# Product-key experts: the first top-k block beside the query projection, operands in PSUM, one expert group kept on chip, rows earlier

## The chip, the cores and the metric

One core of a Trainium2 chip. The metric is device time in microseconds of one execution of the whole program.

## What is computed

The program is two transformer blocks over 512 tokens of width 1024 in f32. Only the last part, `peer_ffn` of the second block, is touched. For each token 8 heads each choose 16 of 16384 single-neuron experts by two top-16 searches over 128 keys and one over the 256 sums of their winners:

```python
q = jnp.einsum('bsd,de->bse', h, w_q).reshape(B, S, PEER_HEADS, PEER_D_KEY)
s1 = jnp.einsum('bshd,hnd->bshn', q[..., :PEER_HALF], keys1)
s2 = jnp.einsum('bshd,hnd->bshn', q[..., PEER_HALF:], keys2)
v1, i1 = lax.top_k(s1, PEER_TOPK)
v2, i2 = lax.top_k(s2, PEER_TOPK)
cand = (v1[..., :, None] + v2[..., None, :]).reshape(B, S, PEER_HEADS, 256)
vals, c = lax.top_k(cand, PEER_TOPK)
e1 = jnp.take_along_axis(i1, c // PEER_TOPK, axis=-1)
e2 = jnp.take_along_axis(i2, c % PEER_TOPK, axis=-1)
expert = e1 * PEER_N_KEYS + e2
gate = jax.nn.softmax(vals, axis=-1)
# per token: act = gelu(h . u_tab[expert]);  out = sum(gate * act * v_tab[expert])
```

## The kernel before, in words

**Two ways for the tokens.** Tokens 128 to 511 (384 of them, `DENSE`) take a dense way: the activations of all 16384 experts are computed, and a gate matrix that is zero off the chosen experts multiplies them. Tokens 0 to 127 take the sparse way: their 128 experts each are fetched as rows of 4 KB per token, 128 rows of the first table (`u_rows`, dot products) and 128 of the second (`v_rows`, weighted sums), one row for each token per fetch (512 KB).

**Weight tiles.** All matrix products run over a list of tiles of 128x1024 f32. SyncE loads tile t into one of 3 places (`raw`) once the low half of tile t-3 is made. ScalarE (or, before the first expert table, GpSimd) copies it rounded into `wH` (L1114), GpSimd subtracts into `wL` (L1628) once tile t-2 is done on TensorE, and TensorE makes 24 products for a tile (high x high, high x low, low x high, 8 parts; L1643 to L1645). The last 256 tiles are the two expert tables, 16 groups of 8 tiles each.

**Order of the work around the change.**
1. *Query projection*, 16 tiles (`wq`), all 512 tokens. VectorE and ScalarE normalise the tokens beside it. All three compute engines meet after it (`E.meet()`).
2. *Top-k stage.* 32 units, one per block of 128 tokens and head. For unit u TensorE makes the key scores (`key_scores`, L909, one unit ahead, released by `tk_read`), and `BESIDE` says how many tiles of the first table it then does. VectorE runs each unit's searches (L1472 to L1486) with the candidate sum at L1479; the last unit of a block also turns choices into expert numbers and gates (L1492 to L1519, with the searches L1501, L1504, L1505 over 2048 elements, twice). After block 0 the rows of the first table can be fetched; from unit 9 on VectorE takes 3 of them at the start of a unit (`take_row`, L1452), 69 in all. Experts and gates of blocks 1 to 3 are turned to expert-major order (`turn_slots`, `keep_slots`).
3. *Gate stage.* 96 steps of 4 tokens: VectorE makes one-hot rows (L1530) and gated one-hot rows (L1533, four per step), TensorE multiplies them (`gate_products`, L948), three banks in turn, and ScalarE copies the product out (L1150); every 8 steps a store of 2 MB goes to memory. Beside them 36 tiles of the first table, 3 per 8 steps, and 28 dot rows.
4. *Rest of the first table*, 6 tiles. Each finished tile of the first table goes through gelu on ScalarE (L1121) and is stored to memory (L1124).
5. *Second table*, 16 groups of 8 tiles. For each expert tile activations (`Ga`, loads of half a group, L1173) and gates (`Gt`, L1166) come back from memory, ScalarE copies the activation to PSUM (L1180), VectorE multiplies (L1557), both split the result into high and low parts (L1203, L1545), one group ahead of TensorE; VectorE adds each finished tile to the tokens (L1564). Beside it come the last 31 dot rows, over the first 23 tiles, and the 128 rows of the second table (L1459), over the next 93.

**Row fetches.** GpSimd issues them (L1619) in its one queue, right behind the low half of the tile that `ROWS_AFTER` names, 3 tiles before the use. There are 6 places; the fetch of row o waits until row o-6 is used:

```python
if o >= ROWS_HELD:
    pool.wait_ge(sems("rows_used"), o - ROWS_HELD + 1)
```

Of the kernel before, what the change touches and what calls it, by code (L numbers as in the profile page):

```python
# [19 lines left out]
P = 128  # L20
# [135 lines left out]
class Chain:  # L156
# [52 lines left out]
def build(nc, a, first=True, second=True):  # L209

    with ExitStack() as ctx:
# [44 lines left out]
        def over(spec, inner=()):  # L256

            with ExitStack() as e:
                got = {n: sb(n, s, d, on=e) for n, s, d in spec}
                for more in inner:  # L260
# [381 lines left out]
        def second_pe(E, products, products_and_sums, parts_ready, one_tile, part_of_tile, rows_tile, turn, h_hi, h_lo):  # L642
# [255 lines left out]
            E.meet()  # L898
# [3 lines left out]
            pe.wait_ge(sems("keys_in"), 16)  # L902

# [1625 lines left out]
```

## Time and profile before

| | us |
|---|---|
| median of 3 runs (3072.8, 3075.3, 5824.1) | 3075.3 |
| the profiled execution | 3079.0 |
| its span | 3077.3 |

| engine | busy us | share of the span |
|---|---|---|
| PE (TensorE) | 2909.5 | 95% |
| DVE (VectorE) | 2064.6 | 67% |
| POOL (GpSimd) | 1758.3 | 57% |
| ACT (ScalarE) | 1008.4 | 33% |

The mean granted clock of TensorE is 0.989. The stages above lie at about 1680 to 1767 us (projection), 1767 to 2172 (top-k), 2172 to 2412 (gates), 2412 to 2445, and 2445 to 3074 (second table).

How to read it: in a row of windows stand the stretch in us and its length; then the busy us, with instructions in brackets, of PE, PEld (weight loads of TensorE, beside its products), DVE, ACT and POOL; then the granted clock, the mean busy share of the 16 DMA engines, and GB/s. A timeline row has its start and duration in us, the engine, the line, the operation and its tiles; in brackets the idle time before it and what ended it. A wait for several things is put down to the last of them.

### The profile page before, as it was taken

How to read it: one execution, taken by the hardware profiler on the slowest of the kernel's cores; microseconds unless marked ns; L12 is line 12 of the kernel's file. 1: busy time of each engine (PE TensorE's matmuls, PEld its weight loads, DVE VectorE, ACT ScalarE, POOL GpSimd, SP SyncE). 2: the span in 40 equal slices, each digit the busy share in tenths (PEclk: the TensorE clock that was granted, in tenths of full speed). 3: DMA queues.
4: the chain of work that ended last, by engine and by line, in shares of the span. 5: the costliest groups of instructions: out<-in, count | busy, mean ns of one | idle time of the engine just before them, and what ended most of it. 6: DMA issues, size and time to landing. Idle time of an engine off the chain costs nothing.

```text
span 3077.3 us, 40592 instructions
## 1 busy us (share of the span) xinstructions
PE 2909.5 (95%) x15510; PEld 2574.9 (84%) x15510; DVE 2064.6 (67%) x3546; ACT 1008.4 (33%) x1596; POOL 1758.3 (57%) x997
## 2 busy tenths in 40 slices
PE   6999999999999999999999999999999899888889
PEld 5777778888787788788888899999999788888889
DVE  7985369994433625755566299999999366666664
ACT  2152222221222422233321132333566434333333
POOL 4636457776654155411156647877544477777775
PEclk9998999999999999999999999999999999999999
DMA  3212222332232022200033348778677899999995
GB/s 137 89 62 89 69 70 95 97 99 94 88 109 76 28 83 88 72 18 15 15 110 104 95 151 295 258 260 280 226 283 276 298 317 335 331 329 332 334 332 178
DMA packets 201521, 509.15 MB, mean 165 GB/s; under 512 B 15600, under 2 KB 98800, under 8 KB 199792
## 3 DMA queue, kind: packets, MB, share of 16 engines
q1 hardware_dynamic: 73008, 262.64, 25.8%
q0 software_dynamic: 36864, 134.23, 11.9%
q10 hardware_dynamic: 91456, 109.68, 11.1%
q8 instruction: 124, 2.03, 0.3%
q14 instruction: 69, 0.57, 0.1%
HBM read 451.97 MB, written 54.53 MB: 165 GB/s over the span
## 4 chain that ended last, share of the span: by engine, by line
PE 63%; POOL 14%; DVE 12%; issue 7%; ACT 2%; DMA 1%; ACTq 0%; DVEq 0%; POOLq 0%; SPq 0%
PE banks L1643 16%; PE banks L1645 15%; PE banks L1644 15%; POOL sb_wL L1628 9%; DVE sb_sq L2356 3%; POOL sb_rows L1619 3%; PE banks L948 3%; PE banks L406 2%; PE banks L822 1%; POOL sb_tmp L1619 1%; PE banks L830 1%; DVE sb_tmp L2366 1%; DVE sb_sq L2354 1%; PE banks L1679 1%; PE banks L1705 1%
## 5 line engine op out<-in xcount | busy, mean ns | idle before, releaser
L1610 POOL TENSOR_TENSOR sb_wL<-sb_raw,sb_wH 128x1024 fp32r<-128x1024 f32 x242 | 588.4, 2431 | 878.9 <-PE banks L1645 817.4
L1643 PE MATMUL banks<-sb_hH,sb_wH 128*128 128x512 f32 (+1 forms) x2040 | 765.5, 375 | 30.3 <-POOL sb_wL L1628 18.7
L1628 POOL TENSOR_TENSOR sb_wL<-sb_raw,sb_wH 128x1024 fp32r<-128x1024 f32 x253 | 624.0, 2468 | 255.9 <-PE banks L1645 247.0
L1644 PE MATMUL banks<-sb_hL,sb_wH 128*128 128x512 f32 (+1 forms) x2040 | 743.3, 364 | 0.0
L1645 PE MATMUL banks<-sb_hH,sb_wL 128*128 128x512 f32 (+1 forms) x2040 | 743.2, 364 | 0.0
L1643 PEld LDWEIGHTS banks<-sb_hH,sb_wH 128*128 128x128 f32 x2040 | 387.1, 190 | 82.5 <-POOL sb_wL L1628 22.1
L1643 PE MATMUL banks<-sb_pzH,sb_wH 128*128 128x384 f32 x1024 | 354.5, 346 | 74.0 <-POOL sb_wL L1628 68.1
L1645 PEld LDWEIGHTS banks<-sb_hH,sb_wL 128*128 128x128 f32 x2040 | 386.2, 189 | 40.8
L1644 PEld LDWEIGHTS banks<-sb_hL,sb_wH 128*128 128x128 f32 x2040 | 387.4, 190 | 38.7 <-issue 1.7
L1114 ACT ACTIVATE sb_wH<-sb_raw 128x1024 fp32r<-128x1024 f32 x253 | 267.3, 1057 | 312.7 <-DMA sb_raw<-in_weights 271.7
L1645 PE MATMUL banks<-sb_pzH,sb_wL 128*128 128x384 f32 x1024 | 345.2, 337 | 0.0
L1644 PE MATMUL banks<-sb_pzL,sb_wH 128*128 128x384 f32 x1024 | 345.0, 337 | 0.0
L1605 POOL TENSOR_SCALAR sb_wH<-sb_raw 128x1024 fp32r<-128x1024 f32 x242 | 305.1, 1261 | 13.0 <-DMA sb_raw<-in_weights 13.0
L1643 PEld LDWEIGHTS banks<-sb_pzH,sb_wH 128*128 128x128 f32 x1024 | 193.6, 189 | 99.7 <-POOL sb_wL L1628 83.2
L1564 DVE TENSOR_TENSOR sb_xT<-sb_xT,banks 128x384 f32<-128x384 f32 x128 | 71.0, 555 | 234.6 <-PE banks L1645 234.2
L1644 PEld LDWEIGHTS banks<-sb_pzL,sb_wH 128*128 128x128 f32 x1024 | 194.1, 190 | 0.0
L1645 PEld LDWEIGHTS banks<-sb_pzH,sb_wL 128*128 128x128 f32 x1024 | 193.7, 189 | 0.0
L1121 ACT ACTIVATE sb_sq<-banks 128x384 f32<-128x384 f32 x128 | 64.8, 506 | 267.1 <-PE banks L1645 262.0
L2356 DVE SCALAR_TENSOR_TENSOR sb_sq<-sb_uab,sb_params,sb_sq 128x512 f32<-128x512 f32 x88 | 145.4, 1652 | 3.1
L1150 ACT ACTIVATE sb_stage<-banks 128x512 f32<-128x512 f32 x96 | 108.7, 1132 | 86.3 <-PE banks L948 84.4
L1533 DVE TENSOR_SCALAR sb_gated<-banks,sb_slots 128x128 f32<-128x128 f32 x384 | 130.6, 405 | 0.0
L1619 POOL DMA_INDIRECT sb_rows<-in_v_rows,sb_idx x86 | 81.3, 946 | 74.3 <-DVE banks L1459 66.7
(456 smaller groups left out, 5222.2 us busy)
## 6 DMA issues: line engine op xcount, KB each, us to landing
sb_raw<-in_weights SPq DMA_DIRECT2D x495, 512.0 KB, 3.6
acts<-sb_sq ACTq DMA_DIRECT2D x128, 192.0 KB, 4.0
gates<-sb_stage ACTq DMA_DIRECT2D x12, 2048.0 KB, 7.9
sb_Ga<-acts ACTq DMA_DIRECT2D x32, 768.0 KB, 7.5
sb_Gt<-gates ACTq DMA_DIRECT2D x32, 768.0 KB, 10.2
acts<-sb_xT ACTq DMA_DIRECT2D x1, 2048.0 KB, 7.8
sb_xT<-acts ACTq DMA_DIRECT2D x1, 2048.0 KB, 10.1
out_xT<-sb_xT ACTq DMA_DIRECT2D x8, 256.0 KB, 2.5
```

The source lines that it names most:

```text
L948: mm = pe.matmul(ps[2 + r][:, x * P:(x + 1) * P], B["gated"][:, i % 4, x], B["onehot"][:, i % 4, x], start=True, stop=True)
L1114: act.activation(wH[:, t % HIS, :], raw[:, t % RAWS, :], ACT.Copy).then_inc(sems("weights_hi"), 1)
L1150: act.activation(stage[:, :, 4 * r:4 * r + 4].rearrange("p e t -> p t e"), ps[2 + i % 3][:, :].rearrange("p (t e) -> p t e", t=4), ACT.Cop ...
L1533: ins = v.tensor_scalar(B["gated"][:, r, x], iota, at(1, x), at(2, x), ALU.is_equal, ALU.mult)
L1605: nc.gpsimd.tensor_scalar(wH[:, t % HIS, :], raw[:, t % RAWS, :], 1.0, 0.0, ALU.mult, ALU.add).then_inc(sems("weights_hi"), 1)
L1610: nc.gpsimd.tensor_tensor(wL[:, t % LOS, :], raw[:, t % RAWS, :], wH[:, t % HIS, :].bitcast(F32), ALU.subtract).then_inc(sems("weights_lo" ...
L1619: nc.gpsimd.indirect_dma_start(out=rows_at[o % ROWS_HELD], out_offset=None, in_=a["u_rows"] if o < P else a["v_rows"], in_offset=bass.Indi ...
L1628: nc.gpsimd.tensor_tensor(wL[:, t % LOS, :], raw[:, t % RAWS, :], wH[:, t % HIS, :].bitcast(F32), ALU.subtract).then_inc(sems("weights_lo" ...
L1643: pe.matmul(out, hi, H, start=start, stop=False)
L1644: pe.matmul(out, hi, L, start=False, stop=False)
L1645: return pe.matmul(out, lo, H, start=False, stop=stop)
L2356: ins = v.scalar_tensor_tensor(out=to, in0=u[:, k:S + k], scalar=PM("ffn_w", wcol + k), in1=to, op0=ALU.mult, op1=ALU.add)
```

## The change

- Units 0 to 6 move beside the projection: `SCORES_BESIDE` places their scores within its tiles, in banks 6 and 7. The meeting after the projection is dropped for single waits. `BESIDE` starts at unit 7 (`FIRST_UNIT`); 87 tiles instead of 86 lie in the top-k stage and 38 instead of 36 in the gate stage.
- One operand of the candidate sum and of the two searches over 2048 moves to PSUM (`first_in_bank`, `iota`, `if12`); each unit has one small copy more for it.
- A gate step makes its rows with three operations over 512 elements, one of them to PSUM (`equal`), instead of one over 512 and four over 128; the products have two banks instead of three.
- 126 instead of 69 dot rows lie in the top-k stage (5 or 6 per unit from unit 9), the last 2 at the start of the gate stage, then 32 rows of the second table; 96 are left for the second table.
- The last group of the first table is taken first in the second (`GROUP_ORDER`); its activations go straight to `Ga` and its gates to `Gt`, and neither is stored or loaded.

```diff
-BESIDE = ((1, 2, 1, 2, 1, 2, 1, 7),) + 3 * ((2, 2, 3, 2, 2, 2, 3, 7),)
-TOPK_TILES = sum(map(sum, BESIDE))
+FIRST_UNIT = 7
+BESIDE = (6,) + 3 * (3, 2, 3, 3, 2, 3, 3, 8)
+TOPK_TILES = sum(BESIDE)
-GATE_TILES = 3 * GATE_STEPS // 8
+GATE_TILES = 38
+SCORES_BESIDE = {(7, 0): 0, (7, 4): 1, (8, 4): 2, (9, 4): 3, (11, 4): 4, (13, 4): 5, (15, 4): 6}
+GROUP_ORDER = [GROUPS - 1] + list(range(GROUPS - 1))
+KEPT = P - 8
-UNIT_DOTS = {u: (3 * (u - 9), 3 * (u - 9) + 3) for u in range(9, 32)}
-GATE_DOTS = [69 + 28 * i // GATE_STEPS for i in range(GATE_STEPS + 1)]
-LATE_ROWS = [97 + 31 * min(i, 23) // 23 if i < 25 else 128 + 128 * min(i - 25, 93) // 93 for i in range(121)]
-DOTS_DONE = 23
+EARLY_DOTS = 126
+UNIT_DOTS = {u: (EARLY_DOTS * (u - 9) // 23, EARLY_DOTS * (u - 8) // 23) for u in range(9, 32)}
+DOTS_DONE = 8
+GATE_ROWS = [EARLY_DOTS + min(i, DOTS_DONE) * (P - EARLY_DOTS) // DOTS_DONE + max(i - DOTS_DONE - 2, 0) * 32 // 86 for i in range(GATE_STEPS + 1)]
+LATE_ROWS = [GATE_ROWS[-1] + (2 * P - GATE_ROWS[-1]) * i // 118 if i < 118 else 2 * P for i in range(121)]
+GATE_AT = [8 * GATE_TILES * (i + 1) // GATE_STEPS - 1 for i in range(GATE_STEPS)]
...
+        work, cand = kept[:, 0, 0:256], kept[:, 0, 256:512]
+        iota, if12 = ps[5][:, 0:P], ps[5][:, P:3 * P].rearrange("p (h c i) -> p h c i", h=8, c=2)
+        v12, first_in_bank = [kept[:, 1, 16 * c:16 * c + 16] for c in range(2)], ps[5][:, 3 * P:3 * P + 16]
...
             def beside_wq(b, k):
+                if (b, k) in SCORES_BESIDE:
+                    first_scores(SCORES_BESIDE[b, k])
...
-            E.meet()
+            first_scores(FIRST_UNIT)
+            E.at("rb_used", E.n["made rb"])
...
-                r = i % 3
+                r = i % 2
                 E.eng.wait_ge(sems("gb_rows"), i + 1)
-                E.at("gb_copied", i - 2)
+                E.at("gb_copied", i - 1)
...
+                if n >= KEPT:
+                    act.activation(B["Ga"][:, n - KEPT, :], bank(t, DN), ACT.Gelu).then_inc(sems(f"bank_free{BANK[t]}"), 1)
+                    weight_hi(t + HIS)
+                    return
...
-                act.activation(stage[:, :, 4 * r:4 * r + 4].rearrange("p e t -> p t e"),
-                               ps[2 + i % 3][:, :].rearrange("p (t e) -> p t e", t=4), ACT.Copy).then_inc(sems("gb_copied"), 1)
+                product = ps[2 + i % 2][:, :].rearrange("p (t e) -> p t e", t=4)
+                act.activation(stage[:, 0:KEPT, 4 * r:4 * r + 4].rearrange("p e t -> p t e"), product[:, :, 0:KEPT], ACT.Copy)
+                act.activation(B["Gt"][:, j, :, 4 * r:4 * r + 4].rearrange("p e t -> p t e"), product[:, :, KEPT:P],
+                               ACT.Copy).then_inc(sems("gb_copied"), 1)
...
+                    if c == 0:
+                        chain.after(v.tensor_copy(first_in_bank, vals))
-                chain(v.tensor_tensor(cand, B["v12"][:, 0].unsqueeze(2).to_broadcast([P, 16, 16]),
-                                      B["v12"][:, 1].unsqueeze(1).to_broadcast([P, 16, 16]), ALU.add))
+                chain(v.tensor_tensor(cand.rearrange("p (i j) -> p i j", i=16), first_in_bank.unsqueeze(2).to_broadcast([P, 16, 16]),
+                                      v12[1].unsqueeze(1).to_broadcast([P, 16, 16]), ALU.add))
...
-                chain(v.tensor_copy(B["if12"][:], B["i12"][:]))
+                chain(v.tensor_copy(if12, B["i12"][:]))
-                                          C("iota", 0, 16).unsqueeze(1).to_broadcast([P, P, 16]), ALU.is_equal))
+                                          iota[:, 0:16].unsqueeze(1).to_broadcast([P, P, 16]), ALU.is_equal))
-                    chain(v.tensor_tensor(e4, e4, B["if12"][:, :, c].unsqueeze(2).to_broadcast([P, 8, 16, 16]), ALU.mult))
+                    chain(v.tensor_tensor(e4, e4, if12[:, :, c].unsqueeze(2).to_broadcast([P, 8, 16, 16]), ALU.mult))
...
+            equal = ps[4][:, :].rearrange("p (x t) -> p x t", x=4)
-                v.tensor_tensor(B["onehot"][:, r], iota.unsqueeze(1).to_broadcast(bc),
-                                B["slots"][:, 0, 4 * i:4 * i + 4].unsqueeze(2).to_broadcast(bc), ALU.is_equal)
-                for x in range(4):
-                    ins = v.tensor_scalar(B["gated"][:, r, x], iota, at(1, x), at(2, x), ALU.is_equal, ALU.mult)
-                ins.then_inc(sems("gb_rows"), 1)
-                for o in range(GATE_DOTS[i], GATE_DOTS[i + 1]):
+                E.at("gb_rows", i)
+                chain.after(v.tensor_tensor(equal, iota.unsqueeze(1).to_broadcast(bc), slot(1), ALU.is_equal))
+                v.tensor_tensor(B["onehot"][:, r], iota.unsqueeze(1).to_broadcast(bc), slot(0), ALU.is_equal)
+                chain.wait()
+                v.tensor_tensor(B["gated"][:, r], equal, slot(2), ALU.mult).then_inc(sems("gb_rows"), 1)
+                for o in range(GATE_ROWS[i], GATE_ROWS[i + 1]):
                     take_row(o)
...
-    peer = [u.reshape(-1, P, D), d.reshape(-1, P, D)]
+    peer = [u.reshape(-1, P, D), d[GROUP_ORDER].reshape(-1, P, D)]
```

## Rows read from the trace of the kernel before

**Rows 1.** Windows of the whole core; the columns are named under time and profile.

```profile
1680.00:1767.00 87.00, 85.95 (x384) 70.52 (x385) 19.23 (x26) 15.19 (x26) 53.93 (x31) 1.00 0.32 102
1767.00:2172.00 405.00, 386.34 (x2226) 382.74 (x2225) 383.63 (x1000) 137.72 (x189) 297.84 (x159) 0.97 0.72 245
2172.00:2412.00 240.00, 237.35 (x1633) 237.00 (x1633) 215.40 (x536) 153.54 (x170) 109.98 (x61) 0.99 0.74 263
2412.00:2452.00 40.00, 32.76 (x172) 30.23 (x170) 7.27 (x14) 16.95 (x29) 22.47 (x13) 0.91 0.98 353
2452.00:3074.00 622.00, 553.65 (x3062) 529.97 (x3062) 378.57 (x562) 235.17 (x369) 446.85 (x279) 0.99 0.91 312
1875.00:1900.00 25.00, 25.00 (x148) 24.81 (x147) 23.66 (x73) 8.73 (x12) 21.96 (x16) 1.00 0.97 352
```

**Rows 2.** Timeline of VectorE: start us, us, line, operation, [idle before <-releaser].

```profile
3070.06 0.56 DVE L1564 TENSOR_TENSOR sb_xT<-sb_xT,banks 128x384 f32<-128x384 f32 x1 [3.61 <-PE banks L1645]
3074.22 0.56 DVE L1564 TENSOR_TENSOR sb_xT<-sb_xT,banks 128x384 f32<-128x384 f32 x1 [3.61 <-PE banks L1645]
```

**Rows 3.** Timeline of ScalarE's queue and of TensorE between the two tables.

```profile
2427.77 6.39 ACTq L1166 DMA_DIRECT2D sb_Gt<-gates  x2
...
2445.43 0.66 PE L1643 MATMUL banks<-sb_pzH,sb_wH 128*128 128x384 f32 x1 [5.36 <-POOL sb_wL L1628]
```

**Rows 4.** Waits, 2475 to 3020: who for whom, us in total, times, longest us.

```profile
POOL sb_rows L1619 <- DVE banks L1459: 66.7, 45, 2.6
PE banks L1643 <- POOL sb_wL L1628: 61.5, 63, 1.3
```

**Rows 5.** Timeline of GpSimd in the second table.

```profile
2634.12 0.94 POOL L1619 DMA_INDIRECT sb_tmp<-in_v_rows,sb_idx  x1 [1.26 <-DVE banks L1459]
2635.07 2.39 POOL L1628 TENSOR_TENSOR sb_wL<-sb_raw,sb_wH 128x1024 fp32r<-128x1024 f32 x1
```

**Rows 6.** Transfers from 2590 to 3010: all queues' packets, and the weight tiles.

```profile
DMA packets 73479, 139.43 MB, mean 332 GB/s; under 512 B 3911, under 2 KB 47661, under 8 KB 73452
...
sb_raw<-in_weights SPq DMA_DIRECT2D x85, 512.0 KB, 6.2
```

**Rows 7.** Gate stage: VectorE's timeline; durations (ns min/median/max, first, last start).

```profile
2296.87 1.21 DVE L1452 SCALAR_TENSOR_TENSOR sb_tmp<-sb_tmp,banks 128x1024 f32<-128x1024 f32 x1
...
2298.00 0.69 DVE L1530 TENSOR_TENSOR sb_onehot<-banks,sb_slots 128x512 f32<-128x512 f32 x1
2298.61 1.36 DVE L1533 TENSOR_SCALAR sb_gated<-banks,sb_slots 128x128 f32<-128x128 f32 x4
2299.89 0.69 DVE L1530 TENSOR_TENSOR sb_onehot<-banks,sb_slots 128x512 f32<-128x512 f32 x1
...
L948 PE MATMUL banks<-sb_onehot,sb_gated x768: 271/275/423, 2176.9 to 2412.4; 128*128 128x128 f32 x192
...
L1530 DVE TENSOR_TENSOR sb_onehot<-banks,sb_slots x96: 682/692/704, 2174.9 to 2402.9; 128x512 f32<-128x512 f32 x96
```

**Rows 8.** Top-k: units 0 and 1 start on VectorE; durations, sum and search.

```profile
1767.46 0.30 DVE L1472 MAX8 sb_v<-banks 128x8 f32<-128x128 f32 x1 [0.47 <-PE banks L909]
...
1774.15 0.30 DVE L1472 MAX8 sb_v<-banks 128x8 f32<-128x128 f32 x1
...
L1479 DVE TENSOR_TENSOR sb_cand<-sb_v x32: 424/466/4381, 1771.2 to 2144.0; 128x256 f32<-128x256 f32 x32
...
L1504 DVE TENSOR_TENSOR sb_eq<-sb_eq,sb_if x8: 2293/4369/4378, 1829.2 to 2162.3; 128x2048 f32<-128x2048 f32 x8
```

**Rows 9.** Timeline of VectorE, its first operation after the projection.

```profile
1766.69 0.29 DVE L1443 COPY banks<-sb_consts 128x128 f32<-128x128 f32 x1 [39.74 <-ACTq L200]
```

**Rows 10.** Row fetches from 1850 to 2170, from issue to landing.

```profile
DMA to landing us min/median/max: 4.7/6.5/7.5
```

**Rows 11.** Timeline of TensorE behind a wait at the end of top-k.

```profile
2166.84 0.51 PE L1643 MATMUL banks<-sb_hH,sb_wH 128*128 128x384 f32 x1 [2.48 <-POOL sb_wL L1628]
2167.15 0.52 PE L1644 MATMUL banks<-sb_hL,sb_wH 128*128 128x384 f32 x1
```

More of the change, by code:

```diff
@@ L92 @@
     for _o in range(_a, _b):
-        ROWS_AFTER[_o] = sum(BESIDE[n // 8][n % 8] for n in range(_u)) - ROWS_AHEAD
+        ROWS_AFTER[_o] = sum(BESIDE[:_u - FIRST_UNIT]) - ROWS_AHEAD
 for _i in range(GATE_STEPS):
-    for _o in range(GATE_DOTS[_i], GATE_DOTS[_i + 1]):
-        ROWS_AFTER[_o] = TOPK_TILES + 3 * _i // 8 - ROWS_AHEAD
+    for _o in range(GATE_ROWS[_i], GATE_ROWS[_i + 1]):
+        ROWS_AFTER[_o] = TOPK_TILES + GATE_AT[_i] // 8 - ROWS_AHEAD
 for _i in range(120):
@@ L161, in __init__, with after, wait, __call__ @@
         self.eng, self.sem, self.n = eng, sem, 0
-    def __call__(self, ins):
+    def after(self, ins):
         ins.then_inc(self.sem, 1)
         self.n = self.n + 1
+    def wait(self):
         self.eng.wait_ge(self.sem, self.n)
+    def __call__(self, ins):
+        self.after(ins)
+        self.wait()
 class Side:
@@ L884, in second_pe, with score_bank, key_scores, first_scores @@
             products("out2", 8, h_hi, h_lo, ready=lambda k: E.wait("merged_parts"))
+            def score_bank(u):
+                return ps[6 + u % 2 if u < 8 else 2 + u % 2]
+            def key_scores(u):
+                tb, h = u // 8, u % 8
+                E.at("tk_read", 2 * (u - 1))
+                for c in range(2):
+                    mm = pe.matmul(score_bank(u)[:, c * P:(c + 1) * P], B["qp"][:, 2 * h + c, tb * P:(tb + 1) * P],
+                                   B["keys"][:, 2 * h + c, :], start=True, stop=True)
+                mm.then_inc(sems("tk_scores"), 1)
+            def first_scores(h):
+                if h == 0:
+                    pe.wait_ge(sems("keys_in"), 16)
+                for c in range(2):
+                    emptied(E, TILE["wq"] + 2 * h + c)
+                key_scores(h)
             def beside_wq(b, k):
+                if (b, k) in SCORES_BESIDE:
+                    first_scores(SCORES_BESIDE[b, k])
                 if b == 0:
@@ L1103, in second_act @@
                     hi_part(E, hH[:, k, :])
-            E.meet()
+            E.at("sq_used", E.n["made sq"])
             t0 = TILE["peer"]
@@ L1132, in second_act @@
             n = 0
-            for u in range(32):
-                for b in range(BESIDE[u // 8][u % 8]):
-                    if b == 3:
+            for u in range(FIRST_UNIT, 32):
+                for b in range(BESIDE[u - FIRST_UNIT]):
+                    if u % 8 == 7 and b == (2 if u == 7 else 4):
                         E.wait("tk_centred")
```

136 lines of the change are left out of this document (64 added, 72 removed).

## The prediction, before the result was known

> **What bounds the kernel now.** First the span by stages [rows 1]; in each row the reader is to see who is busy to the brim. In the query projection (1680 to 1767) TensorE is, while VectorE works 19 of 87 us. In the top-k stage (1767 to 2172, 86 tiles) it is VectorE: 384 of 405 us. In the gate stage (2172 to 2412, 36 tiles, 96 steps) it is TensorE again. From 2412 to 2452 the granted clock is 0.91, and in the second table (2452 to 3074) no engine is full: TensorE 554 of 622 us, VectorE 379, GpSimd 447, with the DMA engines at 0.91.
>
> A tile without waits is read at the end, where adds that each wait for a tile start 4.16 us apart [rows 2]. 128 tiles would be 532 us; the second table takes 629 (from 2445.4, [rows 3], to about 3074). The waits [rows 4] say why: TensorE waits for the low half of the weights (L1628), and GpSimd, which makes it, waits for VectorE's use of rows (L1459, 66.7 us in one of two groups). In GpSimd's queue [rows 5] the row fetch of 2634.12 waits 1.26 us and the weight half stands right behind it. A row is fetched 3 tiles ahead into 6 places; at 128 rows in 93 tiles (1.37) a place's last use lies 4.4 tiles before its next, so the fetch waits for a tile just ended. The tile is 4.94 us there (85 in 420 us, [rows 6]).
>
> **The second table after.** The change leaves it 96 rows over 118 tiles, 0.81 a tile; a place is then used 7.4 tiles before its next use, and the fetch stops waiting. What is late next: GpSimd has 2.4 + 0.81 x 0.95 = 3.2 us a tile [rows 5], VectorE and ScalarE less than now, so the transfers. A tile moves 0.524 MB of weights, 0.393 of activations and gates and 0.43 of rows, 1.34 MB; at the 332 GB/s that this stretch reaches [rows 6] that is 4.05 us, below 4.16, and in [rows 1] a stretch with DMA share 0.97 has TensorE at 25.00 of 25. I take 4.20 us, between 4.16 (nothing shows) and 4.35 (bursts of two 768 KB loads show): 128 x 4.20 = 538 us.
>
> **Between the tables.** Now two gate loads keep ScalarE's queue 6.39 us, and TensorE waits 5.36 us [rows 3]. After, the last group's activations and gates stay in their buffers and that group is taken first: its product, split and transfer to the operand run behind the last three tiles of the first table. I leave 1 us for the last part, gelu to split.
>
> **Gate stage.** The gate products run from 2176.9 to 2412.4 [rows 7]; less 36 tiles that leaves 0.9 us for each of 96 steps. With 38 tiles: 235.5 + 8.3 = 244 us, if TensorE still bounds. VectorE now needs 1.89 us a step (2298.00 to 2299.89) and 1.13 a dot row (2296.87 to 2298.00). After, it has three operations over 512 instead of one and four over 128; one over 512 lets the next start 0.61 us later (2298.00 to 2298.61), so 1.83, and 0.15 for two waits on its own results. With 2 dot rows and 32 rows of the second table, priced at the 1.21 of a dot row's duration, that is 190 + 41 = 231 us, under 244: covered by TensorE. The new operations write or read PSUM on both sides; between no more (0.61) and twice that, only the upper end would bind, by up to 176 us less the cover of 13; I take the row's value, since L1530 already reads PSUM. The gate copy on ScalarE is split in two and has two banks instead of three: it may then be late by two steps, 5 us; covered.
>
> **Top-k on VectorE.** A unit without rows is 1767.46 to 1774.15, 6.69 us, and holds a candidate sum of the shortest kind; over the stage this sum takes 0.42 to 4.38 us, and the search L1504 2.29 to 4.38 [rows 8]. Both have two operands in SBUF. L1530, with one in PSUM, stays at 0.68 to 0.70 in 96 calls [rows 7]. The change puts one operand of each in PSUM, so I take the shortest times: a unit 6.69 plus a small copy of 0.18 (between nothing and a short max of 0.30), 6.87; the end of a block six operations of 2.32 and 2.6 of small ones, 16.5; and 6 us in all for two small operations that keep both operands in SBUF (between nothing and 8 x 4.4).
>
> Units 0 to 6 move beside the projection. VectorE is free there from 1766.69 - 39.74 = 1727.0 [rows 9]; a projection tile is 24 x 87 / 384 = 5.44 us. Scores 2 are due in tile 8 at 1726.0 but need unit 0 read (3.0 us into the unit, 1730.4); scores 3, at 1736.3, need unit 1 (1737.3): TensorE waits 5.4 us. Seven pairs of score products add 7 x 0.45. The first table starts at 1775.6 instead of about 1771, and VectorE starts unit 7 at 1778.8, as the scores of unit 6 come at 1771.9. From there it has 25 x 6.87 + 126 x 1.14 + 4 x 16.5 + 6 = 388 us; TensorE has 87 x 4.16 + 24 x 0.45 + 6 = 379. VectorE still bounds, by little.
>
> **What 57 more rows cost in that stage.** A unit that doesn't end a block has 2.71 tiles and 5.5 rows: VectorE 13.1 us, TensorE 11.7. It moves 2.71 x 0.721 + 5.5 x 0.524 = 4.84 MB: 13.3 us at the 352 GB/s and 0.97 of the dense stretch [rows 1], 14.6 at 332 [rows 6]. I take 13.5, near the first, which is of this stage: 0.4 over VectorE in 20 units, 8 us. The Trainium skill gives a core about 358 GB/s of HBM (DMA: Bandwidth & Descriptors, Specifications). An estimate by that rule is 13.5 us for this unit, no ground to move the sum; the trace's 352 at share 0.97 agrees.
>
> Then the queue. The rows of a unit can be fetched only as those of the unit before are used, and the weight half behind them needs 0.95 + 2.4 us more. TensorE can't come nearer to VectorE than about 9 us at a unit of two tiles and 5 at one of three; being faster it will be there, so the last unit's tiles (8 x 4.16 + 0.45 from 4.7 us after VectorE's start) end 8.6 us after VectorE's work.
>
> **Sum.** VectorE ends top-k at 1778.8 + 388 + 8 = 2174.8, TensorE at 2183.4 (now about 2173). The first gate product comes 4 us later, as now, then 244, three tiles 12.5, and 1: the second table starts at 2444.9, as now, but without the stumbling start. 538 us is 2982.9, and 3.4 from the last product to the end: span 2986 against 3077.3. The profiled execution took 3079.0; the median of the runs shown is 3075.3, 2 under the span. The forecast is **2984 us**, 3.0% less.
>
> **Rivals.**
> - *The top-k stage waits for rows* (16%). For it: three engines within 4% of each other there, six places for 5.5 rows a unit. Against: rows land in 7.5 us at most in that stage [rows 10], and a place has about 13. At 14.6 to 15 us a unit, 20 units cost 22 to 30 more: 3006 to 3014.
> - *The second table stays at the transfers' bound* (10%), at 4.40 us a tile: 26 us more, 3010. For it is the DMA share of 0.91 over the whole stage; against, the 4% below TensorE.
> - *PSUM operands don't help* (9%): the long times of L1479 and L1504 have another cause. By the stage's own 24 sums and the searches, 24 x 0.8 + 6 x 2.1 = 32 us come back: 3016.
> - *Slower* (7%): GpSimd, blocked behind rows that VectorE frees in bursts of 5.5 x 1.14 = 6.3 us, holds the weight half over 8.3 us (two tiles) in the top-k stage. TensorE then stands, and its clock is low after it: behind a wait of 2.48 us its products start 0.32 us apart [rows 11], against 4.16 / 24 = 0.17. 6 us of waiting and 2 of the low clock in 23 units is 184, of which 30 are in my sum: 3138. It decides once VectorE leads TensorE by less than 5 us. Against: scores are made a unit ahead, so VectorE can lead by a unit.
>
> That the rows don't move as said is excluded by the tables in the diff.
>
> **Numbers.** Forecast 58%, its own range 2966 (4.16 a tile, no transfer term) to 3005 (4.30 and 16 us). Faster by over 2%, about what a measurement of this kernel can tell from no change, means under 3013.8: the 58, and half or a little less of the three rivals near that line, 74%. Same 19%, slower 7%. The range 2955 to 3030 leaves out the slow case and ends of the others.
>
> **What would show it.** In the changed profile: adds 4.2 us apart in the second table, GpSimd not waiting for VectorE there, DMA share over 0.95; no gap of TensorE over 2 us between the tables; no candidate sum over 0.5 us; VectorE over 95% busy in top-k. Wrong would be: row products waiting for transfers in top-k, weight halves over 8 us behind fetches, tiles of 4.4 us in the second table.

## The result, and the profile after

The changed kernel takes 3053.3 us (median of 6 runs, 3048.6 to 3058.8) against 3074.1 before: ratio 0.9935, 95% interval 0.9921 to 0.995. (The 3074.1 is a median over six runs too, one of which took 5824.1; the ratio leaves that one out.) That is 0.65% faster, clear of noise by its interval but under the 2% that the prediction counted as a change; the forecast was 3.0%, 2984 us, with a range of 2955 to 3030. The profiled execution took 3053.7, its span is 3051.8.

Three times divide a span: the first gate product, the last one, the end.

| kernel | first gate product | gate stage | last gate product to the end | span |
|---|---|---|---|---|
| before | 2176.9 | 235.5 | 664.9 | 3077.3 |
| forecast | 2187 | 244 | 555 | 2986 |
| after | 2246.3 | 243.9 | 561.6 | 3051.8 |

So 59 of the 66 us by which the span misses the forecast went in the top-k stage and 7 behind the gate stage. Windows of the whole core after: top-k stage, gate stage, the 40 us between the tables, second table [against rows 1].

```profile
1775.00:2242.00 467.00, 412.49 (x2215) 406.16 (x2214) 375.40 (x970) 138.68 (x191) 326.13 (x216) 0.92 0.77 276
2246.00:2490.00 244.00, 243.73 (x1669) 243.74 (x1670) 217.09 (x323) 155.97 (x265) 119.13 (x69) 0.99 0.73 267
2490.00:2530.00 40.00, 31.14 (x165) 30.02 (x165) 15.10 (x27) 20.03 (x37) 21.15 (x12) 0.87 0.83 286
2530.00:3048.00 518.00, 518.00 (x2993) 517.96 (x2992) 291.23 (x455) 229.63 (x355) 383.44 (x215) 1.00 0.88 303
```

In the last row TensorE is never idle; in the first nobody is full: TensorE 412 of 467 us at a clock of 0.92, VectorE 375, GpSimd 326, transfers at 0.77. So here the time goes in waits of one queue for another, and the next step is to find which. The second table and the gate stage came as forecast: adds 4.16 us apart [as rows 2], 128 of them in 530.4 us; candidate sums and searches always at their shortest [rows 8]; the 96 steps of the gate stage with 0.70, 0.68 and 0.68 us for the three operations [rows 7].

VectorE's adds, then durations (ns min/median/max) of the adds, the sum, a search and the gate stage's new operation:

```profile
3044.65 0.55 DVE L1609 TENSOR_TENSOR sb_xT<-sb_xT,banks 128x384 f32<-128x384 f32 x1 [3.61 <-PE banks L1687]
3048.81 0.55 DVE L1609 TENSOR_TENSOR sb_xT<-sb_xT,banks 128x384 f32<-128x384 f32 x1 [3.61 <-PE banks L1687]
...
L1609 DVE TENSOR_TENSOR sb_xT<-sb_xT,banks x128: 553/554/555, 2518.4 to 3048.8; 128x384 f32<-128x384 f32 x128
...
L1518 DVE TENSOR_TENSOR sb_dg<-banks,sb_dg x32: 424/424/426, 1726.9 to 2207.1; 128x256 f32<-128x256 f32 x32
...
L1543 DVE TENSOR_TENSOR sb_eq<-sb_eq,banks x8: 2286/2286/2290, 1789.2 to 2222.5; 128x2048 f32<-128x2048 f32 x8
...
L1571 DVE TENSOR_TENSOR banks<-banks,sb_slots x96: 689/700/700, 2244.3 to 2480.2; 128x512 f32<-128x512 f32 x96
```

What holds the top-k stage is in its waits, 1775 to 2242 (who for whom, us in total, times, longest us):

```profile
POOL sb_wL L1670 <- PE banks L1687: 98.8, 40, 5.1
PEld banks L1685 <- POOL sb_wL L1670: 60.7, 21, 3.9
PE banks L1685 <- POOL sb_wL L1670: 54.5, 21, 3.5
DVE sb_rows L1490 <- DMA sb_rows<-in_u_rows,sb_idx: 37.7, 30, 4.4
POOL sb_rows L1661 <- issue: 18.6, 63, 0.3
DVE sb_tmp L1490 <- DMA sb_tmp<-in_u_rows,sb_idx: 16.2, 14, 4.9
```

TensorE waits 21 times for a low half, up to 3.5 us, about once a unit. VectorE waits 54 us for rows, but GpSimd hardly ever for VectorE. GpSimd's own timeline at one such place, and TensorE's behind it:

```profile
1825.59 2.41 POOL L1670 TENSOR_TENSOR sb_wL<-sb_raw,sb_wH 128x1024 fp32r<-128x1024 f32 x1 [2.28 <-PE banks L1687]
1828.14 0.95 POOL L1661 DMA_INDIRECT sb_tmp<-in_u_rows,sb_idx  x1
1829.40 0.94 POOL L1661 DMA_INDIRECT sb_tmp<-in_u_rows,sb_idx  x1 [0.30 <-issue]
1830.64 0.94 POOL L1661 DMA_INDIRECT sb_rows<-in_u_rows,sb_idx  x1 [0.30 <-issue]
1831.89 0.94 POOL L1661 DMA_INDIRECT sb_rows<-in_u_rows,sb_idx  x1 [0.31 <-issue]
1833.13 0.94 POOL L1661 DMA_INDIRECT sb_rows<-in_u_rows,sb_idx  x1 [0.30 <-issue]
1834.38 0.94 POOL L1661 DMA_INDIRECT sb_rows<-in_u_rows,sb_idx  x1 [0.30 <-issue]
1835.32 4.71 POOL L1670 TENSOR_TENSOR sb_wL<-sb_raw,sb_wH 128x1024 fp32r<-128x1024 f32 x2
```

```profile
1837.75 0.44 PE L1685 MATMUL banks<-sb_hH,sb_wH 128*128 128x384 f32 x1 [3.53 <-POOL sb_wL L1670]
1838.03 0.38 PE L1686 MATMUL banks<-sb_hL,sb_wH 128*128 128x384 f32 x1
1838.20 0.53 PE L1687 MATMUL banks<-sb_hH,sb_wL 128*128 128x384 f32 x1
1838.52 0.53 PE L1685 MATMUL banks<-sb_hH,sb_wH 128*128 128x384 f32 x1
```

The reader is to see that nothing in this burst waits for another engine: the fetches start 1.24 us apart, 0.94 of the record and 0.30 that the trace calls issue. The first low half starts when a tile ends (1825.5); its place in `wL` was the one that tile freed, so TensorE has from there just two tiles and a pair of scores, until 1834.2. GpSimd needs low half, six fetches, low half, until 1837.7. TensorE stands 3.53 us, and 0.45 us later (1838.20) its products start 0.32 us apart instead of 0.17, until 1841.4: the granted clock of that stretch is 0.50, the 1.2 GHz level instead of 2.4.

**Theory A**: GpSimd's queue, a low half behind a burst of fetches, is the cost. **Theory B**: the transfers (266 to 361 GB/s in stretches of this stage, VectorE waiting for rows) are. **Theory D**: something else in the change is. For the 7 us between the tables the question is whether an order or the transfers make them.

### The profile page after: what moved, and what is told of

Same layout as the page of the kernel before. It is cut to its first block, busy times and chain, and to the rows that moved or that the text cites. A ratio compares the mean times of both kernels' runs of the same rounds, so it can differ in the third digit from the quotient of the medians.

```text
span 3051.8 us, 40601 instructions
## 1 busy us (share of the span) xinstructions
PE 2911.1 (95%) x15510; PEld 2598.6 (85%) x15510; DVE 2022.2 (66%) x3386; ACT 1011.1 (33%) x1692; POOL 1735.4 (57%) x997
## 4 chain that ended last, share of the span: by engine, by line
PE 76%; DVE 12%; POOL 5%; issue 4%; ACT 2%; DMA 1%; DVEq 0%; ACTq 0%; SPq 0%; POOLq 0%
PE banks L1685 20%; PE banks L1687 19%; PE banks L1686 19%; DVE sb_sq L2398 3%; PE banks L978 3%; POOL sb_wL L1670 3%; POOL sb_rows L1661 2%; PE banks L839 2%; PE banks L423 1%; PE banks L847 1%; DVE sb_tmp L2408 1%; DVE sb_sq L2396 1%; PE banks L1747 1%; POOL sb_tmp L1661 1%; PE banks L1721 1%
## 5 line engine op out<-in xcount | busy, mean ns | idle before, releaser
L1652 POOL TENSOR_TENSOR sb_wL<-sb_raw,sb_wH 128x1024 fp32r<-128x1024 f32 x242 | 588.5, 2432 | 881.3 <-PE banks L1687 829.9
L1685 PE MATMUL banks<-sb_hH,sb_wH 128*128 128x512 f32 (+1 forms) x2040 | 775.1, 380 | 65.2 <-POOL sb_wL L1670 54.5
L1670 POOL TENSOR_TENSOR sb_wL<-sb_raw,sb_wH 128x1024 fp32r<-128x1024 f32 x253 | 606.5, 2402 | 354.7 <-PE banks L1687 351.2
L1686 PE MATMUL banks<-sb_hL,sb_wH 128*128 128x512 f32 (+1 forms) x2040 | 752.7, 369 | 0.0
L1685 PE MATMUL banks<-sb_pz,sb_wH 128*128 128x384 f32 x1024 | 343.4, 335 | 7.5 <-DVE sb_pz L1590 7.5
L1686 PE MATMUL banks<-sb_pz,sb_wH 128*128 128x384 f32 x1024 | 343.0, 335 | 0.0
L1687 PE MATMUL banks<-sb_pz,sb_wL 128*128 128x384 f32 x1024 | 342.9, 335 | 0.0
L1685 PEld LDWEIGHTS banks<-sb_pz,sb_wH 128*128 128x128 f32 x1024 | 192.9, 188 | 8.4 <-DVE sb_pz L1590 8.4
L1686 PEld LDWEIGHTS banks<-sb_pz,sb_wH 128*128 128x128 f32 x1024 | 192.9, 188 | 0.0
L1687 PEld LDWEIGHTS banks<-sb_pz,sb_wL 128*128 128x128 f32 x1024 | 192.9, 188 | 0.0
L1490 DVE SCALAR_TENSOR_TENSOR sb_rows<-sb_rows,banks 128x1024 f32<-128x1024 f32 x86 | 103.5, 1220 | 40.2 <-DMA sb_rows<-in_u_rows,sb_idx 37.7
L1195 ACT ACTIVATE sb_stage<-banks 128x480 f32<-128x480 f32 x96 | 102.2, 1065 | 82.1 <-PE banks L978 80.5
L1497 DVE SCALAR_TENSOR_TENSOR banks<-sb_rows,sb_row_weights,banks 128x1024 f32<-128x1024 f32 x85 | 109.0, 1282 | 0.0
```

Source lines behind the costliest of these rows:

```text
L1195: act.activation(stage[:, 0:KEPT, 4 * r:4 * r + 4].rearrange("p e t -> p t e"), product[:, :, 0:KEPT], ACT.Copy)
L1490: ins = v.scalar_tensor_tensor(out=row, in0=row, scalar=1.0, in1=row_bank, op0=ALU.mult, op1=ALU.mult, accum_out=B["dots"][:, o:o + 1])
L1497: ins = v.scalar_tensor_tensor(out=row_bank, in0=row, scalar=B["row_weights"][:, o - P:o - P + 1], in1=row_bank, op0=ALU.mult, op1=ALU.add)
L1652: nc.gpsimd.tensor_tensor(wL[:, t % LOS, :], raw[:, t % RAWS, :], wH[:, t % HIS, :].bitcast(F32), ALU.subtract).then_inc(sems("weights_lo" ...
L1670: nc.gpsimd.tensor_tensor(wL[:, t % LOS, :], raw[:, t % RAWS, :], wH[:, t % HIS, :].bitcast(F32), ALU.subtract).then_inc(sems("weights_lo" ...
L1685: pe.matmul(out, hi, H, start=start, stop=False)
```

## The experiments

**e1, a quarter of the bytes.** 

> From row 6 on a fetch moves a quarter of a row for each token (128 KB instead of 512 KB), so the rows' values are wrong and the dot products are multiplied by zero; the number of fetches, their places in GpSimd's queue and VectorE's instructions are those of the changed kernel. Theory A (GpSimd's queue: 5 or 6 fetches at 1.24 us each and then the low half stand in a row, 9.8 us against two tiles' 8.3): the top-k stage (from the scores of unit 7 at 1773 to the last turn at 2242, 469 us) stays within 10 us of 469, TensorE goes on waiting about 3.5 us for a low half once in each unit. Theory B (the transfers, up to 361 GB/s in this stage, hold rows and weight tiles up): the stage loses at least 40 us, and the waits for low halves fall under 20 us in all, from 54. The second table stays at 4.16 us a tile either way, since TensorE was never idle there.

```diff
+                full = rows_at[o % ROWS_HELD]
+                table = a["u_rows"] if o < P else a["v_rows"]
                 nc.gpsimd.indirect_dma_start(
-                    out=rows_at[o % ROWS_HELD], ...
+                    out=full if o < ROWS_HELD else full[:, 0:D // 4], out_offset=None,
+                    in_=table if o < ROWS_HELD else table.rearrange("n (q d) -> (n q) d", q=4), ...
```

One run, 3052.0 us; first gate product 2252.0, last 2495.9. The same window and waits as above:

```profile
1775.00:2242.00 467.00, 408.83 (x2211) 401.72 (x2210) 373.85 (x990) 137.32 (x190) 328.03 (x216) 0.93 0.55 174
...
L1663 POOL DMA_INDIRECT sb_rows<-in_u_rows,sb_idx x86: 941/949/1137, 1807.7 to 2246.6; - x86
...
PE banks L1688 <- POOL sb_wL L1673: 57.4, 21, 3.6
```

174 GB/s instead of 276 and nothing is gained: B falls for this stage, and by waits that stay alike (57.4 and 54.5 us in 21), not only by the time of a single run. A fetch of a quarter costs GpSimd as much, 949 ns against 937. The Trainium skill (Perfetto Trace Analysis, DMA Instruction — SWDGE (GPSIMD)) says that the record of such a DMA ends when its descriptors are generated, not when the data has moved; the trace agrees. Behind the gate stage this kernel needs 554.3 us instead of 561.6, which comes back below.

**e2, the same rows, spread.** 

> The same rows in the same units, but at most two fetches behind the low half of one tile instead of 5 or 6. Theory A (queue): TensorE's waits for low halves fall from 54 us to under 15, the granted clock of the stage rises from 0.92 to over 0.96, the top-k stage falls from 469 us to 400 to 430, the program to 2985 to 3015. Theory B (transfers): as many bytes in as short a time, so the stage stays at 455 to 469 and the program at 3040 to 3055. Rival C: the last fetches of a unit now come too late for VectorE, its waits for rows grow from 54 us, and GpSimd then waits for used places; the stage gains less than 15 us or loses.

```diff
... (against the changed kernel)
-        ROWS_AFTER[_o] = sum(BESIDE[:_u - FIRST_UNIT]) - ROWS_AHEAD
+        ROWS_AFTER[_o] = sum(BESIDE[:_u - FIRST_UNIT]) - ROWS_AHEAD + (_o - _a) // 2
```

Median 2996.0 us of 4 (2990.1 to 3003.4), ratio to before 0.9742 (0.9708 to 0.9777). First gate product at 2183.2, 63 us earlier; window and waits of the stage:

```profile
1775.00:2179.00 404.00, 385.11 (x2187) 378.28 (x2186) 366.99 (x950) 142.10 (x191) 327.14 (x214) 0.98 0.89 318
...
PE banks L1685 <- POOL sb_wL L1670: 18.7, 18, 3.6
```

(The profiled run is the fastest of the four; by the medians the gain is 57 us.) One term in one line is worth 1.9%. A holds, though 18.7 us of waits stay where under 15 were expected; C is out, as VectorE's waits for rows fall from 54 to 16 us. The 18.7 are of the same kind: in six places, where the last fetch of a unit of two tiles meets the first of the next unit, the edit still puts three or four fetches behind one low half and not two, and 14.6 us of the waits end 6 to 9 us after the first fetch of one of these six. Before the longest, 3.56 us at 1854.3, the three fetches start at 1845.93, 1847.19 and, after 2.77 us in which GpSimd waits for VectorE's use of a row, 1850.90.

**e4, no rows moved.** 

> Everything of the change but the rows' move: 69 dot rows in the top-k stage (3 per unit), 28 in the gate stage, 31 dot rows and all 128 rows of the second table beside it, as before the change. Theory A (queue): 3 fetches and a low half are 6.1 us, under two tiles' 8.3; TensorE does not wait, the stage is TensorE's own 87 tiles and scores, 385 to 400 us. Rival D (something else in the change holds the stage up: one operand in PSUM, two banks of scores, 8 tiles in the last unit): it stays above 430 us. The second table goes back to about 4.9 us a tile, 620 to 628 us, so the program is near 3050 either way under A (70 to 80 us gained in top-k, 80 to 85 lost in the second table: 3040 to 3065) and near 3110 to 3130 under D.

```diff
-EARLY_DOTS = 126
-DOTS_DONE = 8
+EARLY_DOTS = 69
+DOTS_DONE = 23
-GATE_ROWS = ...
-LATE_ROWS = ...
+GATE_ROWS = [69 + 28 * i // GATE_STEPS for i in range(GATE_STEPS + 1)]
+LATE_ROWS = [97 + 31 * min(i, 23) // 23 if i < 25 else 128 + 128 * min(i - 25, 93) // 93 for i in range(121)]
```

with `row_weights` made at step 8 + 23 + 1 of the second table, as before the change. Median 3046.9 of 4, ratio 0.9908 (0.9875 to 0.994); first gate product 2155.2, last 2399.0, 646.1 from there to the end.

```profile
1775.00:2151.00 376.00, 375.25 (x2196) 371.98 (x2196) 302.24 (x843) 140.03 (x191) 273.88 (x157) 1.00 0.77 263
...
PE banks L1685 <- POOL sb_wL L1670: 0.7, 3, 0.3
DVE sb_rows L1490 <- DMA sb_rows<-in_u_rows,sb_idx: 31.8, 24, 4.9
DVE sb_tmp L1490 <- DMA sb_tmp<-in_u_rows,sb_idx: 7.7, 9, 1.8
```

TensorE is busy in 375.25 of 376 us at full clock, D is out, and VectorE waits 39.5 us for rows all the same: here it is early, and that wait costs nothing. In the traces the rows' move costs 91.1 us before the gate stage (2155.2 to 2246.3) and brings 84.5 behind it (646.1 to 561.6): as it was done, the largest part of the change lost 7 us. (The medians say the same, 3046.9 against 3053.3, but their intervals overlap: whether it lost a little or nothing is not shown.) The rest of the change moved the first gate product from 2176.9 to 2155.2.

**e6 and e7, the size of the burst.** 

> Only how many rows stand in one burst is changed: 92 dot rows in the top-k stage, 4 per unit, all behind one low half; 34 dots in the gate stage, 2 dots and all 128 rows of the second table beside it, so only the top-k stage is read. Theory A: 4 fetches and a low half are 4 x 1.24 + 2.4 = 7.4 us, still under two tiles' 8.3, so TensorE waits under 5 us in the stage and the first gate product is at 2155 to 2160. Rival E (the rows cost in proportion to their number, 91 us for 57 rows more): 23 rows more than 69 cost 37 us, 2192.

```diff
-EARLY_DOTS = 69
+EARLY_DOTS = 92
-GATE_ROWS = [69 + 28 * i // GATE_STEPS ...
-LATE_ROWS = [97 + 31 * min(i, 23) // 23 ...
+GATE_ROWS = [92 + 34 * i // GATE_STEPS ...
+LATE_ROWS = [126 + 2 * min(i, 23) // 23 ...
```

(against e4.) 

> 115 dot rows in the top-k stage, 5 in every unit's burst (the changed kernel: 11 units of 5 and 12 of 6); 13 dots and 26 rows of the second table in the gate stage, 102 beside the second table. Theory A: 5 x 1.24 + 2.4 = 8.6 us against 8.3, so each burst costs TensorE a wait of 0.3 to 2 us and now and then its clock; first gate product at 2175 to 2215. Rival E (proportional): 2155.2 + 46 x 1.6 = 2229.

```diff
-EARLY_DOTS = 126
-DOTS_DONE = 8
+EARLY_DOTS = 115
+DOTS_DONE = 24
```

One run of each, 3061.4 and 3028.7 us in all. TensorE's waits for low halves from 1775 to 2246, e6 and then e7, in a fence each:

```profile
PE banks L1685 <- POOL sb_wL L1670: 21.9, 23, 1.5
```

```profile
PE banks L1685 <- POOL sb_wL L1670: 42.5, 21, 2.7
```

| rows in a burst | waits, us | longest | 2 x 2.4 + 1.24 r - 8.32 | first gate product | later than e4 |
|---|---|---|---|---|---|
| 3 (e4) | 0.7 | 0.3 | 0.2 | 2155.2 | |
| 4 (e6) | 21.9 | 1.5 | 1.4 | 2188.2 | 33 |
| 5 (e7) | 42.5 | 2.7 | 2.7 | 2222.2 | 67 |
| 5 or 6 (after) | 54.5 | 3.5 | 2.7 or 3.9 | 2246.3 | 91 |

Here my own sum was wrong: with one low half in it (7.4 us against 8.3) four fetches should have been free, and I expected 2155 to 2160 for e6 and 2175 to 2215 for e7. The timeline above has two low halves in the two tiles, the one before the burst and the one behind it; with both the sum, made after these runs, gives the longest wait of e4, e6 and e7 and that of the changed kernel to 0.4 us. Rival E, in proportion to the rows, gave 2192 and 2229 and was nearer to the time, but e2 refutes it as a cause: 57 rows more than e4, spread, cost 28 us instead of 91 (34 by e2's median).

The waits are 21, 42 and 54 us more than e4's, and 12, 25 and 37 us are left over. In e7 and in the changed kernel most of that is the low clock behind the waits: the stage's clock is 0.95 and 0.92, and 131 and 187 products start 0.32 us apart instead of 0.17, which makes 19 and 27 us. In e6, whose waits are 1.5 us at most, the clock is 1.00 and not one product does; its 12 us are something else. About half is the restart of each wait: round one of 1.07 us (1837.73) the products' starts are 1.41 us apart, and the next 0.28, where 0.17 is the rule, so 0.28 us more are lost than the wait shows: 6 us in 23 waits, and about as much in e7, where it closes the sum (19 + 6 for 25). What is left, some 6 us in e6 and 4 in the changed kernel, is open.

**e3, two orders between the tables.** 

> Two orders are changed between the tables: ScalarE copies the kept activations up before it makes the next weight tile's high half, and VectorE makes the low part of expert tile 7 before it waits for the gates of the next group. If the two waits of TensorE of 3.8 us each at 2511.9 and 2517.0 came from these orders, both vanish, the program is 8 to 12 us shorter (ratio to the changed kernel 0.996 to 0.997) and the clock in the 25 us after is at its full value. If they come from the load of the gates or the weight tile itself (the transfers), the waits stay and move by less than 1 us; then the program is the same within 2 us.

```diff
... (ScalarE; early_gelu(n, False) leaves out its weight_hi)
-                    while n < 8 * GROUPS and n <= KEPT + m + 2:
-                        early_gelu(n)
-                        n += 1
+                    late = n < 8 * GROUPS and n <= KEPT + m + 2
+                    if late:
+                        early_gelu(n, False)
+                        n += 1
                     if m + 2 < 8 * GROUPS:
                         act_up(m + 2)
+                    if late:
+                        weight_hi(t0 + n - 1 + HIS)
... (VectorE; the weighted_lo(m - 1) further down is left out for m == 8)
+                if m == 8:
+                    weighted_lo(7)
                 if z < GROUPS:
                     if z and e % 4 == 0:
                         E.eng.wait_ge(sems(f"gates_in{e // 4}"), 16 * z)
```

Median 3044.9 of 4, ratio 0.9903 (0.987 to 0.9937), which overlaps that of the changed kernel. In the traces, from the last gate product to the end, 556.5 us instead of 561.6; the other 5.8 us of the two traces' difference lie before the first gate product, which this edit does not touch. So the 8.4 us between the medians, which would fit the 8 to 12 expected, are not all the edit's: 5 are seen where it works. After had two waits in its first tile of the second table (first fence, with a window of 10 us ahead of them); the second fence is e3's, which has one:

```profile
2500.00:2510.00 10.00, 8.12 (x47) 7.80 (x45) 2.04 (x4) 5.24 (x10) 7.53 (x5) 1.00 1.00 367
...
2508.80 1.06 ACT L1148 ACTIVATE sb_wH<-sb_raw 128x1024 fp32r<-128x1024 f32 x1 [3.28 <-DMA sb_raw<-in_weights]
...
2511.89 0.69 PE L1685 MATMUL banks<-sb_pz,sb_wH 128*128 128x384 f32 x1 [3.77 <-DVE sb_pz L1590]
2517.00 0.69 PE L1685 MATMUL banks<-sb_pz,sb_wH 128*128 128x384 f32 x1 [3.77 <-DVE sb_pz L1590]
```

```profile
2503.27 1.06 ACT L1148 ACTIVATE sb_wH<-sb_raw 128x1024 fp32r<-128x1024 f32 x1 [3.06 <-DMA sb_raw<-in_weights]
...
2505.35 0.44 PE L1691 MATMUL banks<-sb_pz,sb_wH 128*128 128x384 f32 x1 [3.07 <-DVE sb_pz L1594]
```

Half of each theory: the order of VectorE cost one wait; the other stays, since ScalarE's next split stands behind a high half whose raw tile has not landed, while the transfers are full (the window of after, share 1.00). e1, with the old orders and fewer bytes, has 554.3, and its two waits there are 2.17 and 0.36 us. So these orders cost what they do because the transfers are full there.

**e5, rows divided by GpSimd's room.** 

> Rows are divided by GpSimd's room: 116 in the top-k stage (4 per unit, 12 in a block's last unit), of a unit's fetches at most two behind one low half, VectorE takes them in twos and fours between the searches; 34 in the gate stage (12 dots, then 22 rows), 106 beside the second table; the two orders of e3 are in it. Theory A (GpSimd's queue per block: 27 low halves at 2.4 us and 40 fetches at 1.24 us are 114 us, under TensorE's 118): TensorE waits under 8 us in the top-k stage, first gate product at 2155 to 2170 (with 69 rows 2155.2, with 126 spread rows 2183.2), gate stage 244 us, second table 556.5 us after the last gate product plus 0 to 10 for ten rows more there: 2958 to 2980. Theory B (transfers hold the stage up once rows and tiles come together, up to 361 GB/s): first gate product at 2175 to 2190, waits for low halves or for raw tiles of 15 us and more, 2980 to 2995.

```diff
+TOPK_ROWS = {u: 12 if u % 8 == 7 else 4 for u in range(9, 32)}
-EARLY_DOTS = 126
+EARLY_DOTS = sum(TOPK_ROWS.values())
-DOTS_DONE = 8
+DOTS_DONE = 32
-...max(i - DOTS_DONE - 2, 0) * 32 // 86...
+...max(i - DOTS_DONE - 2, 0) * 22 // 62...
-        ROWS_AFTER[_o] = sum(BESIDE[:_u - FIRST_UNIT]) - ROWS_AHEAD
+        ROWS_AFTER[_o] = sum(BESIDE[:_u - FIRST_UNIT]) - ROWS_AHEAD + (_o - _a) * BESIDE[_u - FIRST_UNIT] // (_b - _a)
```

with `take_rows(2)` before a unit's searches, 2 after them, and in a block's last unit 4 after each of its two searches over 2048. The two orders of e3 are in it. Median 2962.0 of 5 (2959.1 to 2967.2), ratio 0.9644 (0.9631 to 0.9658).

```profile
1775.00:2162.00 387.00, 382.72 (x2241) 381.03 (x2240) 363.97 (x970) 143.99 (x193) 323.97 (x209) 1.00 0.91 323
...
L979 PE MATMUL banks<-sb_onehot,sb_gated x768: 272/275/418, 2165.6 to 2409.5; 128*128 128x128 f32 x192
...
2560.00:2800.00 240.00, 240.00 (x1386) 240.00 (x1385) 148.03 (x227) 108.79 (x173) 188.00 (x111) 1.00 0.96 334
```

3.6% less than before, 3.0% less than the changed kernel. TensorE waits 3.5 us for low halves in the whole stage, with at most two fetches behind any one and transfers at 323 GB/s: A. The end is 555.5 us behind the last gate product.

**e8, its operands back in SBUF.** 

> e5 with the operands of the candidate sum and of the two searches over 2048 back in SBUF. By the rows of before against those of the changed kernel VectorE loses 0.5 us on each of 23 sums and 2.1 us on each of 6 pairs of searches, 24 us in the stage. If VectorE still has room beside TensorE (with 69 rows it was busy 169 of 200 us), the program is within 6 us of e5; if VectorE and GpSimd now lie on TensorE's path because GpSimd's low halves are also held while VectorE reads, first gate product 15 to 30 us later than in e5.

```diff
... (against e5)
-                        chain.after(v.tensor_copy(first_in_bank, vals))
-first_in_bank.unsqueeze(2)...    iota[:, 0:16].unsqueeze(1)...    if12[:, :, c].unsqueeze(2)...
+v12[0].unsqueeze(2)...           C("iota", 0, 16).unsqueeze(1)... B["if12"][:, :, c].unsqueeze(2)...
```

Median 2995.2 of 4, ratio 0.9762 (0.9745 to 0.9779): 33 us slower than e5. First gate product 2195.6 against 2165.6. Durations of the sum, then waits from 1775 to 2145:

```profile
L1528 DVE TENSOR_TENSOR sb_dg<-sb_dg x32: 424/1717/2285, 1724.2 to 2151.2; 128x256 f32<-128x256 f32 x32
...
PE banks L1700 <- POOL sb_wL L1685: 23.1, 10, 7.9
POOL sb_rows L1676 <- DVE sb_rows L1495: 16.4, 7, 8.5
POOL sb_tmp L1676 <- DVE sb_tmp L1495: 12.2, 3, 8.5
```

The sum's median goes from 0.42 to 1.72 us, VectorE falls behind, and now GpSimd does wait for used places, up to 8.5 us, with low halves behind it, for which TensorE then waits up to 7.9 us. PSUM operands are worth 30 us here; in e4 VectorE has 74 of 376 us free, so it was not measured what they are worth there. The Trainium skill (SBUF — State Buffer, SBUF: two separate sides) says that a VectorE operation with two SBUF inputs and a GpSimd operation that reads SBUF exclude each other for a whole instruction; the sums agree with it: 424 ns at the shortest and 2285 at the longest, 1.86 us more, which is under the 2.4 us of one low half.

**e9, fewer rows at the end.** 

> e5 with 6 rows fewer in unit 31 (6 instead of 12), taken beside the second table instead (112 there); the rest as in e5. In e5 TensorE waits once, 3.4 us, for a low half and once, 2.6 us, for the gated rows near 2150, and its first gate product is at 2165.6 against 2155.2 with 69 rows. If VectorE's 6 rows of 1.3 us in unit 31 hold the last experts and gates up, the first gate product comes 5 to 9 us earlier, 2157 to 2161, and the second table stays at TensorE's 4.16 us a tile: 2953 to 2958, ratio to e5 0.997 to 0.999. If 112 rows there are past what the transfers carry (0.96 of their time was used with 106 rows), the second table takes 5 us or more longer, and the time is that of e5 or worse.

```diff
... (against e5)
-TOPK_ROWS = {u: 12 if u % 8 == 7 else 4 for u in range(9, 32)}
+TOPK_ROWS = {u: 4 + (8, 8, 2)[u // 8 - 1] * (u % 8 == 7) for u in range(9, 32)}
```

The profiled run did a little more than expected: first gate product 2154.4, 11 us earlier, 2953.2 us. But the five runs go from 2953.2 to 2968.8, median 2967.0, ratio 0.9652 (0.9639 to 0.9666), that of e5. Four of five have a mean clock of 0.992 to 0.995 where the profiled one has 0.998; only that one has a trace. So the 11 us rest on one trace of each kernel, e5's from the slower end of its five runs and e9's from the fastest; whether the edit gains anything there, and what takes it back, is open.

**e10, more beside the second table.** 

> e5 with 101 rows in the top-k stage (7 instead of 12 in a block's last unit), 34 in the gate stage and 121 beside the second table; only the second table is read. A tile there moves 1.05 MB of weights, activations and gates (524 + 197 + 197 KB are 0.92 MB) and 121/118 rows of 524 KB, 1.455 MB in all. If the transfers' bound is the 332 to 337 GB/s at which the second table of before ran, that is 4.32 to 4.38 us a tile against TensorE's 4.16, and the stretch from the last gate product to the end is 19 to 27 us longer than in e5 (about 555). If TensorE's bound holds still (345 GB/s and more can be had), it is within 5 us of e5's. First gate product at 2155 to 2162 either way.

```diff
... (against e5)
-TOPK_ROWS = {u: 12 if u % 8 == 7 else 4 for u in range(9, 32)}
+TOPK_ROWS = {u: 7 if u % 8 == 7 else 4 for u in range(9, 32)}
-DOTS_DONE = 32
+DOTS_DONE = 48
-...* 22 // 62...
+...* 7 // 46...
```

(The "1.05 MB" of the expectation is a slip; its sum goes by the 0.92.) One run, 2956.5 us; from the last gate product at 2398.3 to the end at 2954.7 are 556.4.

```profile
2560.00:2800.00 240.00, 239.48 (x1382) 239.16 (x1381) 156.86 (x233) 110.76 (x174) 195.70 (x118) 1.00 0.99 351
```

121 rows, 351 GB/s, and TensorE still busy 239.5 of 240 us. The 332 GB/s of [rows 6] were what a stretch full of waits reached, no bound of the transfers. At 0.99 this one is at its end.

## Why the prediction was wrong

1. **The step that failed** is "What 57 more rows cost in that stage". It took the largest of VectorE (13.1 us a unit), TensorE (11.7) and transfers (13.5) and charged 8 us. GpSimd was not in the comparison: its term in this stage was put at nothing. Behind the sum, under "Then the queue", the low half is said to need 0.95 + 2.4 us more, one fetch in front of it, where the change puts five or six there. The 0.95 is the duration of the record; the 0.30 between fetches was not read, since [rows 5] shows a single one. The top-k stage of before has it, in its waits from 1767 to 2172: `POOL sb_rows L1619 <- issue: 8.3, 31, 0.3`. Summed, GpSimd needs 2.71 x 2.4 + 5.5 x 1.24 = 13.3 us a unit, level with the rest, so even the corrected sum would not have shown it. What does is the order inside a unit: 5 or 6 fetches behind one low half cost 91 us against e4 (e6 and e7: 4 cost 33, 5 cost 67); the same fetches, mostly two at a time, 28 (e2). VectorE, which the sum took for the bound and wanted over 95% busy, was busy 375 of 467 us, 80%.
2. **The queue** was then looked at only for blocking by VectorE, there and in the rival "slower". That rival had the right place (a low half held over two tiles) and the right follow-up (the clock), but asked for VectorE to be late and for 8.3 us behind the fetches alone. With two low halves of 2.4 in those 8.3, the room for fetches is 3.5 us, not quite three. It priced 8 us a unit; measured are 4.0 (91 over 23 units). Its condition, VectorE's lead, played no part except in e8.
3. **The rival "waits for rows"** named a sign that did show, 54 us of VectorE waiting for landings. e1 and e4 show it as a follow-up: with a quarter of the bytes it stays, and at full speed of TensorE 39.5 us of it are there.
4. **Between the tables** 1 us was left. The first product of the second table did come about in time (2504.84, 14.6 us behind the last gate product for the 13.5 of the sum), but two later parts of the same tile came 3.77 us late each; with the low clock behind them the first tile's add comes 13.5 us after that product, where a tile has 4.2. Some 3 us come back in the other 127 tiles, so 7 are seen. The step missed that a high half waiting for its raw tile stands ahead of the kept group's parts in ScalarE's queue, and the wait for the next group's gates ahead of the last low part in VectorE's (e3).
5. **Right**: 4.16 to 4.20 us a tile in the second table (530.4 over 127); the gate stage (243.9 for 244); the wait in the projection (5.2 for 5.4); all sums and searches at their shortest, worth 30 us in e8 where 32 were priced; GpSimd free of VectorE in the second table; the transfers there, 324 GB/s from 2560 to 2800 (at a share of 0.94, just under the 0.95 named). With the burst mended, the span of e2's profiled run is 2988.3 against the 2986 of the sum. That is partly luck: it is the fastest of four, their median is 2996.0 against the forecast's 2984, and in it a first gate product 4 us early makes up for part of what is lost between the tables.

## What to carry to other kernels

When work is moved into a stage, add up every queue that it passes, issue time between instructions included, and then look at one unit's order: how long may this queue be away from what the bound engine needs next? A burst that fits on the mean costs its excess every time, and here, with 5 or 6 fetches in it, about half as much again in TensorE's clock. Before giving up the placement of extra transfers, try to spread their issue: here one line brought back 63 us of a stage in the traces, 57 us of the program by the medians, and made a change worth 0.65% one worth 2.6%.

## What was not expected of the hardware

- Row fetches issued by GpSimd back to back start 1.24 to 1.26 us apart, with 512 KB (after) as with 128 (e1): 0.94 to 0.95 us of record and 0.30 in front of the next. Between a low half and a fetch lie 0.15.
- By the table of bursts TensorE lost 1.5 to 1.7 times the sum of its waits. Where the longest was 2.7 and 3.5 us (e7 and after), most of the surplus is products 0.32 us apart behind the waits (stage clock 0.95 and 0.92); where it was 1.5 us (e6) the clock stayed at 1.00, and the surplus has other causes.
- Transfers with row fetches among them reached 351 GB/s over 240 us with TensorE busy in 239.5 of them (e10).
